# Four short GpSimd subtractions instead of one long one, and one last stage instead of four

## The reference, cut to what matters

```
x = x + swiglu(h, w_gate, w_up, w_down)            # twice, in the first block
...
ffn = _hier_moe(_modulate(x, sh2, sc2), ...)       # 32 experts: down(silu(x gate) * (x up)) * share
x = _layernorm(ALPHA * x + g2 * ffn, ln2_g, ln2_b) # the end of the program
```

## Time and profile before

| | |
|---|---|
| Median of 3 runs | 3542.35 us |
| Profiled execution, its own time | 3539.44 us |
| Span of the profiled execution | 3537.7 us |
| Mean granted TensorE clock | 0.945 |
| PE busy | 3121.3 us (88%) |
| DVE busy | 2003.2 us (57%) |
| ACT busy | 1284.0 us (36%) |
| POOL busy | 908.9 us (26%) |
| DMA moved | 439.35 MB, mean 124 GB/s |

### The profile page before, as it was taken

How to read it: one execution, slowest core, us unless ns; L and a number is a source line. 1 busy time by engine, 2 the same in 40 slices (tenths; PEclk the granted TensorE clock), 3 DMA queues, 4 the chain that set the end, 5 groups by cost and what they waited for, 6 DMA issues and landing times. The chain is left out here.

```text
span 3537.7 us, 53372 instructions
## 1 busy us (share of the span) xinstructions
PE 3121.3 (88%) x21792; PEld 2453.9 (69%) x21792; DVE 2003.2 (57%) x2748; ACT 1284.0 (36%) x1614; POOL 908.9 (26%) x472
## 2 busy tenths in 40 slices
PE   7868999998999978999989998389997869999993
PEld 5446887796777756887768776278884358888872
DVE  3656552301333345553299747775544369899984
ACT  2543321221333332332132223312222247777772
POOL 3013443333222213443322210000100014445430
PEclk9989999999999989999989998699998989999996
DMA  3622222322111102222221100501002159999992
GB/s 136 238 108 84 95 95 84 123 86 73 70 54 54 60 24 96 95 95 83 95 84 60 48 17 1 198 3 51 27 27 87 36 191 361 360 369 372 371 357 101
DMA packets 76462, 439.35 MB, mean 124 GB/s; under 512 B 14832, under 2 KB 17904, under 8 KB 27376
## 3 DMA queue, kind: packets, MB, share of 16 engines
q1 hardware_dynamic: 66768, 427.12, 32.5%
q0 software_dynamic: 9504, 9.47, 0.8%
HBM read 421.85 MB, written 39.85 MB: 131 GB/s over the span
## 5 line engine op out<-in xcount | busy, mean ns | idle before, releaser
L76 POOL TENSOR_TENSOR ring_lo<-ring,unit_hi 128x2048 fp32r<-128x2048 f32 x116 | 536.2, 4624 | 1212.0 <-ACT unit_hi L71 1212.0
L122 PE MATMUL wide<-h_hi,unit_hi 128*128 128x512 f32 x1296 | 520.9, 402 | 100.7 <-DVE h_lo L182 44.5
L124 PE MATMUL wide<-h_hi,ring_lo 128*128 128x512 f32 x1296 | 520.2, 401 | 0.0
L123 PE MATMUL wide<-h_lo,unit_hi 128*128 128x512 f32 x1296 | 519.6, 401 | 0.0
L3039 DVE TENSOR_TENSOR ex_w_lo<-ring,ex_w_hi 128x2048 fp32r<-128x2048 f32 x192 | 437.6, 2287 | 44.0 <-ACT ex_w_hi L2992 42.1
L2992 ACT CAST ex_w_hi<-ring 128x2048 fp32r<-128x2048 f32 x192 | 365.4, 1908 | 109.2 <-DMA ring<-in_weights 93.1
L71 ACT CAST unit_hi<-ring 128x2048 fp32r<-128x2048 f32 x116 | 220.3, 1900 | 462.5 <-PE wide L124 453.6
L122 PEld LDWEIGHTS wide<-h_hi,unit_hi 128*128 128x128 f32 x1296 | 251.5, 194 | 179.6 <-POOL ring_lo L76 70.9
L123 PEld LDWEIGHTS wide<-h_lo,unit_hi 128*128 128x128 f32 x1296 | 247.6, 191 | 53.5 <-issue 0.2
L124 PEld LDWEIGHTS wide<-h_hi,ring_lo 128*128 128x128 f32 x1296 | 247.5, 191 | 53.1
L363 DVE TENSOR_TENSOR ffn_hidden_lo<-ffn_whole,ffn_hidden_hi 128x512 f32 (+1 forms) x44 | 201.5, 4579 | 50.6 <-ACT ffn_hidden_hi L338 50.6
(11 more groups left out here) (532 smaller groups left out, 6165.9 us busy)
## 6 DMA issues: line engine op xcount, KB each, us to landing
ring<-in_weights SPq DMA_DIRECT2D x356, 1024.0 KB
factors<-rp_out SPq DMA_DIRECT2D x8, 1536.0 KB, 5.5
rw_F<-factors SPq DMA_DIRECT2D x12, 1024.0 KB, 5.2
cb_both<-pair_rows_out SPq DMA_DIRECT2D x4, 1024.0 KB, 4.8
x<-in_x SPq DMA_DIRECT2D x1, 2048.0 KB, 7.6
x_kept<-x SPq DMA_DIRECT2D x1, 2048.0 KB, 11.7
x<-x_kept SPq DMA_DIRECT2D x1, 2048.0 KB, 8.6
x_mixing<-x SPq DMA_DIRECT2D x1, 2048.0 KB, 7.9
```

The lines of the kernel that those rows point to most:

```text
L76: pool.tensor_tensor(self.lo[n % RING][:, :], self.ring[n % RING][:, :], self.hi[n % 2][:, :].bitcast(F32), ALU.subtract).then_inc(lo_read ...
L122: pe.matmul(dst, a[0], b[0], start=start, stop=False)
L123: pe.matmul(dst, a[0], b[1], start=False, stop=False)
L124: return pe.matmul(dst, a[1], b[0], start=False, stop=stop)
```

## The change

1. `write_lo` issues four instructions of 512 columns for each unit instead of one of 2048. The semaphore is raised by the last of them.
2. In the experts stage the last expert's two down units are split in step 31, after the `silu` (ACT) and the product with the up half (DVE) of that step, and no longer at the head of step 32. On both engines they now stand ahead of expert 30's copy of results and of the split of expert 31's hidden rows.
3. One block, `tail_stage`, takes the place of `combine_stage`, `last_residual_stage`, the last `layer_norm_stage` and the store. The four loads are issued one behind the other, each with a semaphore of its own. The transposes go to bank k of PSUM for feature chunk k (all 512 tokens of a chunk side by side), DVE's residual reads the bank, and there is no `y`. ALPHA x is made by ACT at the start. PE sums chunk k when chunk k's residual is there. The norm is the class `Norm`, which the kernel has already: DVE subtracts the mean straight from the sums in PSUM, ACT squares into two buffers in turn, and each finished chunk of 256 KB is stored at once.

```
@@ -73,8 +73,10 @@
     def write_lo(self, pool, hi_ready, lo_ready, j, i):
         n = self.at + i
         pool.wait_ge(hi_ready, j * RING + (i + 1))
-        pool.tensor_tensor(self.lo[n % RING][:, :], self.ring[n % RING][:, :],
-                           self.hi[n % 2][:, :].bitcast(F32), ALU.subtract).then_inc(lo_ready, 1)
+        for piece in range(4):
+            part = slice(piece * T, (piece + 1) * T)
+            ins = pool.tensor_tensor(self.lo[n % RING][:, part], self.ring[n % RING][:, part], self.hi[n % 2][:, part].bitcast(F32), ALU.subtract)
+        ins.then_inc(lo_ready, 1)
...
@@ -2996,7 +2998,7 @@ (ACT; DVE the same with lo)
                 def step(e, j2, s):
-                    if s >= 1:
+                    if 1 <= s < EXPERTS:
                         for n in range(2):
                             hi(e, down_at(s - 1, n))
...
+                    elif s == EXPERTS - 1:
+                        for n in range(2):
+                            hi(e, down_at(s, n))
                     if s >= 1:
                         g = s - 1
...
+def tail_stage(nc, c, route, pair_rows, x, gate, scale, shift, out):
...
+            @block.sync
+            def _(sp):
                 for t in range(TT):
                     sp.dma_start(both[:, t, :, :].rearrange("p n d -> p (n d)"),
+                                 pair_rows[2 * P * t:2 * P * (t + 1), :].rearrange("(p n) d -> p (n d)", n=2)).then_inc(loaded[t], 16)
+                for k in range(DC):
+                    sp.wait_ge(norm.placed, k + 1)
+                    sp.dma_start(out[:, k, :], x[:, k, :]).then_inc(stored, 16)
+                sp.wait_ge(stored, 16 * DC)
+
+            @block.scalar
+            def _(act):
+                for m in range(DC):
+                    act.mul(x[:, m, :], x[:, m, :], ALPHA).then_inc(grown, 1)
+                norm.scalar(act)
 
             @block.vector
             def _(dve):
                 for t in range(TT):
+                    dve.wait_ge(loaded[t], 16)
...
+                for k in range(DC):
+                    dve.wait_ge(turned, k + 1)
+                    dve.wait_ge(grown, k + 1)
+                    dve.scalar_tensor_tensor(out=x[:, k, :], in0=c.bank[k], scalar=gate(k), in1=x[:, k, :], op0=ALU.mult,
+                                             op1=ALU.add).then_inc(added, 1)
+                norm.vector(dve)
 
             @block.tensor
             def _(pe):
                 for t in range(TT):
                     pe.wait_ge(summed, t + 1)
                     for k in range(DC):
+                        mm = pe.transpose(c.bank[k][:, t * P:(t + 1) * P], both[:, t, 0, k * P:(k + 1) * P], c.ident[:, :])
+                        if t == TT - 1:
                             mm.then_inc(turned, 1)
+                for k in range(DC):
+                    pe.wait_ge(added, k + 1)
+                    norm.sum_chunk(pe, k)
+                pe.wait_ge(added, 2)
+                norm.sum_squares(pe)
```

More of the change, by code:

```diff
@@ L3059, in step @@
                         lo(e, gate_up_at(s + 1, 2))
+                    elif s == EXPERTS - 1:
+                        for n in range(2):
+                            lo(e, down_at(s, n))
                     if s >= 1:
@@ L3079, in experts_stage, with sb @@
     w.at += ALL
-def combine_stage(nc, c, route, pair_rows, y):
+def tail_stage(nc, c, route, pair_rows, x, gate, scale, shift, out):
     with ExitStack() as ctx:
-        both = ctx.enter_context(nc.sbuf_tensor("cb_both", [P, TT, 2, D], F32))
-        loaded, scaled, summed, turned, low_done, high_done = c.semaphores("cb", ("loaded", "scaled", "summed", "turned", "low_done", "high_done"))
+        def sb(n, shape):
+            return ctx.enter_context(nc.sbuf_tensor(f"tail_{n}", shape, F32))
+        both, squares, rstd = sb("both", [P, TT, 2, D]), sb("squares", [P, 2, T]), sb("rstd", [P, T])
+        norm = Norm(c, x, x, x, scale, shift, c.bank[0], c.bank[1], squares, rstd[:, :])
+        fresh = norm.use(c.semaphores("tail", [f"norm_{n}" for n in Norm.NAMES] + [f"loaded{t}" for t in range(TT)] + [
+            "grown", "scaled", "summed", "turned", "added", "stored"]))
+        loaded, (grown, scaled, summed, turned, added, stored) = fresh[:TT], fresh[TT:]
         with nc.Block() as block:
@@ L3103, in _ @@
                                              op0=ALU.mult, op1=ALU.add).then_inc(summed, 1)
-                for t in range(TT):
-                    dve.wait_ge(turned, 2 * t + 2)
-                    dve.tensor_copy(y[:, 4:8, t * P:(t + 1) * P], c.wide[t][:, T:D].rearrange("p (k t) -> p k t", k=4)).then_inc(high_done, 1)
+                for k in range(DC):
[4 more added lines that the diff above has]
+                norm.vector(dve)
             @block.tensor
@@ L3112, in _ @@
                     for k in range(DC):
-                        mm = pe.transpose(c.wide[t][:, k * P:(k + 1) * P], both[:, t, 0, k * P:(k + 1) * P], c.ident[:, :])
-                        if k % 4 == 3:
+                        mm = pe.transpose(c.bank[k][:, t * P:(t + 1) * P], both[:, t, 0, k * P:(k + 1) * P], c.ident[:, :])
+                        if t == TT - 1:
                             mm.then_inc(turned, 1)
-            @block.scalar
-            def _(act):
-                for t in range(TT):
-                    act.wait_ge(turned, 2 * t + 1)
-                    act.copy(y[:, 0:4, t * P:(t + 1) * P], c.wide[t][:, 0:T].rearrange("p (k t) -> p k t", k=4)).then_inc(low_done, 1)
-def last_residual_stage(nc, c, x, y, gate):
-    grown, added = c.semaphores("lres", ("grown", "added"))
-    with nc.Block() as block:
-        @block.scalar
-        def _(act):
-            for m in range(DC):
-                act.mul(x[:, m, :], x[:, m, :], ALPHA).then_inc(grown, 1)
-        @block.vector
-        def _(dve):
-            for m in range(DC):
-                dve.wait_ge(grown, m + 1)
-                dve.scalar_tensor_tensor(out=x[:, m, :], in0=y[:, m, :], scalar=gate(m), in1=x[:, m, :],
-                                         op0=ALU.mult, op1=ALU.add).then_inc(added, 1)
+                for k in range(DC):
[3 more added lines that the diff above has]
+                norm.sum_squares(pe)
 def load_stage(nc, pairs, name):
@@ L3262, in second_block @@
         experts_stage(nc, c, w, route, tokens, pair_rows)
-        combine_stage(nc, c, route, pair_rows, dev)
-        last_residual_stage(nc, c, x, dev, at(5))
-        layer_norm_stage(nc, c, x, x, T, col("ln2_g"), col("ln2_b"), "ln2")
         if upto == 10:
             return dump(x)
-        stored = nc.alloc_semaphore("output_stored")
-        with nc.Block() as block:
-            @block.sync
-            def _(sp):
-                sp.dma_start(out, x[:, :, :]).then_inc(stored, 16)
-                sp.wait_ge(stored, 16)
+        tail_stage(nc, c, route, pair_rows, x, at(5), col("ln2_g"), col("ln2_b"), out)
 COLS = {}
```

5 lines of the change are left out of this document (1 added, 4 removed).

## The result

| | before | changed |
|---|---|---|
| Median | 3541.15 us (4 runs, 3538.79 to 3547.79) | 3495.26 us (4 runs, 3494.59 to 3499.63) |
| Profiled execution, its own time | 3539.44 us | 3494.59 us |
| Span | 3537.7 us | 3492.8 us |
| Mean granted clock | 0.945 | 0.951 |
| POOL busy | 908.9 us | 1018.2 us |

The ratio is 0.9870 with a 95% interval of 0.9853 to 0.9887: 46 us faster, where 34 had been forecast.

What follows compares the result with a forecast made beforehand. TensorE was busy 88% of the span, so gains lay in its waits and the clock behind them; the experts were held by DMA. Terms -8.7 - 3.3 - 21.6 = -33.6 us gave 3507 us, range 3497 to 3520.

Steps and rivals of the forecast that it cites:

- the tail: After the last expert: overlapped loads and sum -15.4, norm -2.0, store -4.2; together -21.6 us (-17 to -24).
- the last expert: Down units split earlier: TensorE's wait before the last down product shrinks 2.5 us, clock adds -0.8; -3.3 (-1.9 to -5).
- the four pieces: GpSimd's subtraction in quarters lets VectorE in sooner where TensorE waits for it: -8.7 us (-13 to -3).
- Rival 3: Transfers do not overlap, in tail loads and stores: 3526 us, or 3520 with the stores alone; chance 0.10.
- The middles of the SwiGLU stages: TensorE's 7.21 us wait for the last hidden rows shortens by 3.2 us in each of two stages, -6.4.
- A piece: One GpSimd subtraction of 512 columns: taken as 1.2 us, between 1156 and 1296 ns, making a unit 4.8 us.
- the sign that I had named: The forecast would be wrong if TensorE's waits at the stage starts grew by over 1 us each.
- The starts and the norm: Output projection starts -1.8 together, norm ahead of the projection -1.5, starts waiting for GpSimd's units +1, beside the convolution 0.
- The projection: Beside the convolution TensorE waits for low parts; the shared port's time stays the same, so taken as 0.
- rival 2: Part one gives more: shortened pauses keep the clock high and gaps beside the convolution close; 3498 us, chance 0.10.
- Rival 1: Only the tail gains, or VectorE waits for all four queued pieces: part one +3, total 3519 us; chance 0.14.
- part one: The forecast's section on the four pieces, -8.7 us; quotes the rule that one engine holds the port for a whole instruction.

Runs made afterwards that it cites:

- its repeat: The changed kernel run again with no edit: 3494.91 us against 3538.92 for the kernel before, ratio 0.9870.
- filler run: Kernel before plus extra matmuls with unread results in the pauses inside the stage starts and the norm's sum, no pieces: 3533.58 us, ratio 0.9983.
- four-piece run: Kernel before plus only the split of each GpSimd unit into four pieces: 3522.86 us against 3539.73, ratio 0.9953.

## Why the prediction was wrong

The direction, the large part and the order of the terms were right: the tail is half of it, the pieces a good third, the last expert the rest. The time fell out of the range because one term, the four pieces, was sized by half: -8.7 us (bounds -13 and -3), measured -16.9 by its own run. The cause that was left out of it is the clock behind a pause.

- *The tail: -21.6, measured -22.7 in the profile and -21.4 by its own run.* Right, term by term: sum -16.5 (forecast -15.4), norm -1.8 (-2.0), store -4.5 (-4.2). The four loads landed 2.5 us apart instead of 2.9, 1.3 us better at the end, while the sum's own 16 instructions took 8.03 us instead of 7.4. Rival 3 is out: the stores of 256 KB each took 2.0 us from issue to landing and were issued 0.7 apart, so only the last one's is seen. The advice of the Trainium skill ("DMA: Bandwidth & Descriptors", "Measured (HBM→SBUF, 128 partitions, SWDGE, issued from GpSimd)") to batch to 1 MiB, whose table is of loads that GpSimd issues, does not bear on a store that would otherwise wait for its data: eight small ones ended 4.5 us sooner than one large.
- *The last expert: -3.3 (-1.9 to -5), measured -5.6, and -0.9 in its own run's profile.* Both lie outside the bounds. The wait fell by 3.3 us in the changed kernel where I had worked out 2.5: the low parts began earlier than I had reckoned and were done before the copy of results could start, not 1.4 us behind it. That TensorE would keep its clock I had at -0.8; where the load was in time, it was -2.3.
- *The middles of the SwiGLU stages: -3.2 each, measured -3.23 in every profile with four pieces.* That is the pause alone. The half clock behind it lasted 2.8 and 5.5 us before, 3.4 and 3.4 in the changed kernel and 4.8 and 4.9 in its repeat: no gain that comes again.
- *A piece: 1.2 us, bounds 1156 and 1296; measured 1376 on average.* Wrong, and past the 1.35 us that I had named as a sign of being wrong; it did not matter much. Alone a piece takes 1.26 us and the next starts 1.22 after it, as estimated. In turn with VectorE it is 1.71, because it waits for VectorE's instruction too. I had let only VectorE wait. TensorE started 1.1 us later at both output projections, also past the sign that I had named. The later starts at the value projection (+1.0) and the second attention (+0.4) lie within the +1 to +3.4 that I had allowed.
- *The starts and the norm: -1.8, -1.5, +1 and 0, measured -5.0, -5.05, -1.7 and, from the norm to the scan, -2.45.* This is the step that failed. I wrote for the output projections that TensorE "stalls 1.89 us after its first unit" and counted the pause by its length. (The row was misread, too: the pause comes after nine of the unit's 48 instructions, inside the start.) For the norm I wrote that TensorE needs "1.7 us for a chunk at the low clock", throughout. The clock was in both cases taken over from the trace of before. But in the trace before the half clock behind the pause was itself a consequence of the pause. When the pause went, TensorE reached full clock while still in its first chunks, 5.3 us after its start instead of 11.9 (windows above). The filler run shows it without any pieces: 2.65 and 1.52 us at the output projections and 2.48 at the norm come back when the pause stays and TensorE is merely kept at work in it. At the norm the other half, and at the SwiGLU starts everything, is the pause itself.
- *The projection: 0, measured -4.1 up to the gates in all five profiles with four pieces and no wait.* "The port's time is the same" failed here. TensorE waited 7.0 us for GpSimd's low parts instead of 9.2 (and 16.8 with eight pieces), and the clock was better, too: a stretch of 3.4 us at half clock behind the wait at 1994 us is gone, and one of 6.8 us at the gates is 3.4. How the 4.1 us are shared between the two is open; the filler run, with whole units, has -1.60 there.

I had the row for it: the earlier trace rows shows a sum at 0.50 and then at 0.98, and rival 2 said that a shortened pause leaves the clock high. Its 3498 us came nearest to the result. But I gave the clock 3 us in all and the rival a chance of 0.10, as a bonus and not as a part of each term. Of the 11.3 us between the forecast of -33.6 and the profiles' -44.9, the starts, the norm and the projection make -12, the last expert -2.3, the tail -1.1; the scan's +4.7 goes against them. In these two profiles chance hid a part of the miss: without the scan's +4.7, which did not come again, it would have been 16 us. Rival 1 is out by the four-piece run and by the 1.34 us above. (The Trainium skill's rule, as part one quotes it, speaks against that rival, not against "the second" as I wrote there.)

*What stays open.* Against the profile of before, the scan stage came out between -0.8 and +4.7 us in the twelve others, and at +4.5 in that of the tail alone, which has the same code up to there. The second attention with its projection moved in the same way, between -2.6 and +3.3 us. In the changed kernel's profile the scan's first part lost clock that the same instructions had in the kernel before. Changed kernel:

```profile
2321.50:2379.50 58.00, 55.15 (x1146) 47.41 (x1144) 32.35 (x70) 13.17 (x33) 5.66 (x12) 0.94 0.01 3
2379.50:2439.50 60.00, 59.37 (x1364) 51.33 (x1360) 33.91 (x76) 14.93 (x37) 5.66 (x12) 1.00 0.12 40
```

Kernel before, at the same instructions:

```profile
2342.00:2400.00 58.00, 55.16 (x1230) 47.28 (x1228) 33.16 (x72) 13.59 (x34) 5.66 (x12) 1.00 0.05 15
2400.00:2460.00 60.00, 58.95 (x1350) 50.92 (x1347) 33.88 (x76) 14.79 (x37) 5.67 (x12) 1.00 0.11 40
```

The same pause of 2.85 us stands at the head of both, and one was followed by half clock and the other not. Another 2 us went at 0.99 to 1.00, for which I have no cause. That it is chance is what the repeat suggests (-0.06), not more.

## What to carry to other kernels

Before a pause of the matrix engine is priced by its length, look at the granted clock behind it: where the engine comes back at half clock, the pause costs its length and, by estimate, half of the time that the half clock lasts behind it. At the first output projection here a pause of 1.89 us had another 2.65 us of clock behind it. Where two engines block each other, ask also whether one of them needs to run then at all: at the norm, one wait that moved GpSimd's two units behind VectorE's eight instructions gave 6.3 us where splitting them gave 5.0. But the splitting went on to give 4.1 us in the projection behind, where the wait gave nothing, so look past the place itself. If splitting, try several numbers: here two pieces left pauses (3501 us), eight made GpSimd late (3507), and four were best (3495).

## What the hardware showed that I had not expected

- Taking turns blocks both. In a run of turns GpSimd's piece of 512 columns took 1.71 to 1.74 us and VectorE's subtraction 1.75 to 1.78, against 1.26 and 0.69 alone; each pair takes 1.68 us from start to start, less than the 1.26 + 0.69 that they take alone.
- GpSimd's subtraction alone takes 0.72 us for 256 columns, 1.26 for 512, 2.34 for 1024 and 4.50 for 2048 (shortest of each): about 0.18 us and 2.1 ns a column.
- Four loads of 1 MB in flight landed 2.5 us apart, 420 GB/s, where the experts' stream ran at 357. From issue to landing they took 4.8 to 11.0 us (median 7.9), where one at a time takes 4.8, and yet the last was there 7 us sooner than when they were loaded one by one.
